# Identity products of TensorE placed in its waits, in a two-block network on one core

## What is computed

```
# first block, per layer
mod = silu(c) @ w_mod + b_mod                 # shifts, scales and gates, 6 x 1024 columns
h   = x * (1 + scale1) + shift1               # latent and context tokens
y   = mixer(h)                                # layer 0: mLSTM scan and attention, layer 1: gated linear attention
x   = layernorm(ALPHA * x + gate1 * y)
f   = peer(x * (1 + scale2) + shift2)         # product-key experts, 16384 of them
x   = layernorm(ALPHA * x + gate2 * f)
# second block, per layer
h   = rmsnorm(x, g_pre)
x   = x + rmsnorm(mixer2(h), g_post)
x   = x + rmsnorm(ffn(rmsnorm(x, g_ffn_pre)), g_ffn_post)
```

## Time and profile before

| | us |
|---|---|
| median of 3 runs | 4111.04 |
| the three runs | 4105.31, 4111.04, 4121.91 |
| the profiled execution, its time | 4121.83 |
| its span, first to last instruction | 4120.1 |
| PE busy in the span | 3940.9 (96%) |
| DVE busy | 3032.1 (74%) |
| ACT busy | 1819.4 (44%) |
| mean granted clock of PE | 0.978 |

### The profile page before, as it was taken

The page is one execution under the profiler, slowest core; times in us unless marked ns, Lnnn a source line. Parts: engine busy times, 40 slices in busy tenths (PEclk is TensorE's granted clock), DMA queues, the critical chain, the costliest instruction groups (busy, mean ns, idle before and its releaser), DMA issues. The chain is left out here.

```text
span 4120.1 us, 66400 instructions
## 1 busy us (share of the span) xinstructions
PE 3940.9 (96%) x25970; PEld 3522.6 (85%) x25970; DVE 3032.1 (74%) x6800; ACT 1819.4 (44%) x2915; POOL 5.9 (0%) x18
## 2 busy tenths in 40 slices
PE   7997999999999999999989999999999789998999
PEld 5766999998888999988868789999888787988798
DVE  3556797778886877788975469777888767756875
ACT  3343444443334444443434344444333544555454
POOL 0000000000000000000000000000000000000000
PEclk8998999999999999999988999999999899999999
DMA  5143575566666865567641247655677422442143
GB/s 214 54 164 123 176 230 180 169 198 240 244 229 257 318 240 168 172 231 256 244 178 70 86 173 231 202 169 176 234 247 245 158 100 77 184 174 107 72 169 143
DMA packets 121684, 752.17 MB, mean 183 GB/s; under 512 B 15712, under 2 KB 17248, under 8 KB 56992
## 3 DMA queue, kind: packets, MB, share of 16 engines
q1 hardware_dynamic: 121376, 747.93, 51.8%
HBM read 693.88 MB, written 54.00 MB: 182 GB/s over the span
## 5 line engine op out<-in xcount | busy, mean ns | idle before, releaser
L1863 DVE TENSOR_TENSOR expert_ring_low<-expert_ring,expert_high 128x1024 fp32r<-128x1024 f32 x768 | 936.1, 1220 | 244.1 <-ACT expert_high L2097 243.8
L2097 ACT ACTIVATE expert_high<-expert_ring 128x1024 fp32r<-128x1024 f32 x768 | 811.9, 1057 | 629.4 <-PE ps L2036 626.0
L2005 PE MATMUL ps<-peer_hT_high_peer,expert_high 128*128 128x256 f32 x3072 | 882.2, 287 | 1.2 <-DVE expert_ring_low L1863 1.0
L2007 PE MATMUL ps<-peer_hT_high_peer,expert_ring_low 128*128 128x256 f32 x3072 | 861.0, 280 | 0.0
L2006 PE MATMUL ps<-peer_hT_low,expert_high 128*128 128x256 f32 x3072 | 860.8, 280 | 0.0
L2005 PEld LDWEIGHTS ps<-peer_hT_high_peer,expert_high 128*128 128x128 f32 x3072 | 583.2, 190 | 3.3 <-DVE expert_ring_low L1863 2.5
L2006 PEld LDWEIGHTS ps<-peer_hT_low,expert_high 128*128 128x128 f32 x3072 | 584.0, 190 | 0.0
L2007 PEld LDWEIGHTS ps<-peer_hT_high_peer,expert_ring_low 128*128 128x128 f32 x3072 | 578.8, 188 | 0.0
L2036 PE MATMUL ps<-expert_high,weighted_high 128*128 128x512 f32 x1536 | 474.5, 390 | 5.8 <-DVE weighted_low L1893 5.8
L2036 PE MATMUL ps<-expert_high,weighted_low 128*128 128x512 f32 x1536 | 474.4, 390 | 0.0
L2036 PE MATMUL ps<-expert_ring_low,weighted_high 128*128 128x512 f32 x1536 | 473.8, 390 | 0.0
(11 more groups left out here) (645 smaller groups left out, 7086.7 us busy)
## 6 DMA issues: line engine op xcount, KB each, us to landing
expert_ring<-in_peer_u SPq DMA_DIRECT2D x192, 1024.0 KB, 5.3
expert_ring<-in_peer_v SPq DMA_DIRECT2D x192, 1024.0 KB, 4.9
gelu_peer<-gelu_out SPq DMA_DIRECT2D x186, 256.0 KB, 5.5
gelu_in_peer<-gelu_peer SPq DMA_DIRECT2D x93, 512.0 KB, 5.7
weight_ring<-in_ffn_w_up SPq DMA_DIRECT2D x22, 2048.0 KB, 7.4
weight_ring<-in_w_in SPq DMA_DIRECT2D x14, 2048.0 KB, 7.4
weight_ring<-in_w_mod SPq DMA_DIRECT2D x12, 2048.0 KB, 7.3
weight_ring<-in_peer_wq SPq DMA_DIRECT2D x12, 2048.0 KB, 7.3
```

The costliest lines, as they stand in the source:

```text
L1863: dve.tensor_tensor(piece(low, n), piece(raw, n), high[:, n % LEAD, :].bitcast(F32), ALU.subtract).then_inc(low_done, 1)
L2005: pe.matmul(o, b[:, s], hT_h[:, c, :], start=(c == 0), stop=False)
L2007: mm = pe.matmul(o, lo[:, s], hT_h[:, c, :], start=False, stop=(c == DC - 1))
L2097: act.activation(high[:, n % LEAD, :], piece(raw, n), ACT.Identity).then_inc(high_done, 1)
```

## The change

A helper `keep_going` is added. It issues n products of the identity with itself, 128 by 128 by 128 in float32, each with start and stop set, into the first 128 columns of a PSUM bank whose content nobody reads any more. It is called on TensorE's list at these places:

- in `Modulation`, 8 before each unit's wait for its transfer, 40 more before the last unit, and 4 after the last sums (8 x 4 + 40 + 4 = 76);
- in `transpose_in`, after the transposes and a wait for the first chunk's copies: 58 in both "h1" stages, 34 in "hn";
- in `Mlstm.weighted`, before the last pair's wait for its weights: 50; and after the weave of `mixer_ab`: 44;
- in `MixOut`, at the end of TensorE's list: 22 per tile, that is 88 with four tiles and 44 with two;
- in `peer_experts`, at the end where `end.cols` isn't empty (two of the three): 86;
- in `rms_in`, as its only TensorE work: 40.

Nothing is removed or reordered otherwise.

```diff
@@ -323,7 +323,13 @@
-def transpose_in(nc, G, name, src, tiles, dst, scale=None, shift=None, loads=(), whole=None, moves=()):
+def keep_going(pe, G, bank, n):
+
+    for _ in range(n):
+        pe.matmul(G.ps[:, bank, 0:P], G.ident[:, :], G.ident[:, :], start=True, stop=True)
+
+
+def transpose_in(nc, G, name, src, tiles, dst, scale=None, shift=None, loads=(), whole=None, moves=(), idle=0):
@@ -342,7 +348,9 @@
                         mm = pe.transpose(ps[:, c, k * P:(k + 1) * P], src(t, c), G.ident[:, :])
                     mm.then_inc(turned, 1)
-
+                if idle:
+                    pe.wait_ge(v_out, pairs)
+                    keep_going(pe, G, 0, idle)
@@ -416,6 +424,7 @@
             def parts(u):
+                keep_going(pe, G, 0, 8)
                 ws.wait_landed(pe, self.u0 + u)
@@ -441,9 +450,12 @@
             parts(0)
             for u in range(1, N):
+                if u == N - 1:
+                    keep_going(pe, G, 0, 40)
                 parts(u)
                 sums(u - 1)
             sums(N - 1)
+            keep_going(pe, G, 0, 4)
@@ -1047,6 +1059,9 @@
                 yield self.t(n) + 5.4 + 0.9 * t
                 if t == 0:
+                    if n == len(self.combos) - 1:
+                        pe.wait_ge(S.qk_out, 4 * H_M)
+                        keep_going(pe, self.G, 2, 50)
                     pe.wait_ge(S.w_ready, 4 * (n + 1))
@@ -1349,6 +1364,8 @@
     def tensor(self, pe):
         yield from merged(self.turn(pe), self.rows(pe), self.products(pe))
+        pe.wait_ge(self.S.cat_low, 2 * len(self.tiles))
+        keep_going(pe, self.G, 4, 22 * len(self.tiles))
@@ -1504,7 +1521,7 @@
             hT_at = nc.sbuf_base - 2 * DC * TOK * 4
             transpose_in(nc, G, "h1", lambda t, c: G.x[:, t, c * P:(c + 1) * P], [0, 1, 2, 3], hT,
-                         scale=lambda c, q: G.mod[:, DC + c, q:q + 1], shift=lambda c, q: G.mod[:, c, q:q + 1])
+                         scale=lambda c, q: G.mod[:, DC + c, q:q + 1], shift=lambda c, q: G.mod[:, c, q:q + 1], idle=58)
             highs = sbuf(nc, "pieces_high", [P, 2, DC, PIECE], F32R)
@@ -1607,6 +1624,8 @@
                     weave(in1.tensor(pe), gates.tensor(pe), rope.tensor(pe), attention.tensor(pe), scan.tensor(pe),
                           mods.tensor(pe))
+                    pe.wait_ge(S.qk_out, 4 * H_M)
+                    keep_going(pe, G, 2, 44)
@@ -2083,6 +2102,9 @@
             products_v(N_KEYS - 2, 1).then_inc(pv_done, 1)
             products_v(N_KEYS - 1, 1).then_inc(pv_done, 1)
+            if end.cols:
+                pe.wait_ge(rows_out, 2 * len(end.cols))
+                keep_going(pe, G, 0, 86)
@@ -2880,6 +2902,10 @@
                    loads=loads) as (
                 block, squared, step_sem, ms_ready, rms_ready, scale_ready, scaled):
+            @block.tensor
+            def _(pe):
+                keep_going(pe, G, 0, 40)
+
             @block.vector
@@ -2911,7 +2937,7 @@
         g = sbuf(nc, "norm_cols", [P, DC], F32)
         rms_in(nc, G, xn, [(g[:, :], G.d[key]), *loads])
-        transpose_in(nc, G, "hn", lambda t, c: xn[:, t, c * P:(c + 1) * P], [0, 1], hT, scale=lambda c, q: g[:, c:c + 1])
+        transpose_in(nc, G, "hn", lambda t, c: xn[:, t, c * P:(c + 1) * P], [0, 1], hT, scale=lambda c, q: g[:, c:c + 1], idle=34)
```

## The result

The changed kernel takes 4165.38 us (median of 4 runs, 4161.06 to 4169.27) against 4109.62 for the kernel before (4 runs, 4105.31 to 4121.91). The ratio is 1.0133, with a 95% interval of 1.0114 to 1.0151: slower by 56 us, where +52 was forecast. The profiled execution took 4169.27 us. Two executions of the kernel before in a later job took 5436 and 8108 us, at a mean granted clock of 0.67 and 0.62; they are in the slow state and left out of every comparison.

A forecast was written before the change was run, and what follows sets the result against it. The prediction took the kernel to be bound by TensorE, busy in 96% of the span. Overruns less clock gains summed to +50.2 us, 4161.2 from the median 4111.04; it took 4163 us, range 4138 to 4184.

The forecast's parts named there:

- One product costs 0.224 us: Each added identity product is two TensorE records of 0.112 us at full clock; 664 products take 149 us.
- the eight overruns: Products outlasting their waits delay stages at the edited places, from +2.9 us in `load_x` to +16.4 from third peer to "hn".
- The scan's line: Scan of `mixer_ab`: groups of 50 and 44 products overrun their waits; together +6.7 us, start of `mix_out` included.
- the -0.5: Start of `mix_out` in `mixer_ab`: better clock gains only 0.5 us, ScalarE being nearly full there.
- Rival 3: Overrun half hidden, other engines starting the next stage while PE finishes: 4153 us; chance 0.87 together with the forecast.
- The gains by the clock: Work behind the filled waits runs at full instead of half clock; 16 us taken, about 19 counted full.
- `mixer_c`'s `In1` (-2.2): Behind "h1" of `mixer_c`, 4.36 us of work at 0.50 would run at full clock, gaining 2.2 us.
- `mixer_2` (-2.0): Start of `mixer_2`: 4.04 us of work at 0.50 would run at full clock, gaining 2.0 us.
- The stretch of 23.89 us: From 2167.36, PE busy at 0.50, costing 11.9 us; read as coming and going, its products untouched by the change.
- Rival 1: At one record, 0.112 us, per product all groups fit their waits and only gains stay: 4095 us; chance 0.10.
- Rival 2: Identity products don't hold the clock, each taking about 0.4 us, gains lost: about 4297 us; chance 0.03.
- The signs: Profile after: about 1328 records of 0.112 us, PE ending stages 6 to 8 us after DVE, clock 1.00 behind edited places.

The follow-up runs named there:

- e3_double: The changed kernel with every group of identity products at twice its length (1328 products): 4314.77 us, ratio 1.0484 to the kernel before.
- wide pair: e9_wide_after compared with e5, which differ by the change alone, both with gate products reading 128 rows: 54.1 us apart.
- e9_wide_after: The changed kernel with `mixer_c`'s eight gate products reading 128 rows, zero-padded, in place of 17: 4161.89 us, ratio 1.0097 to the kernel before.
- e8_h1_only: The kernel before with the 58 identity products in both "h1" stages and nothing else: 4124.58 us, ratio 1.0015.
- e2_one_record: The changed kernel with its 664 identity products issued as transposes, one record each: 4112.05 us, ratio 0.9987 to the kernel before.
- e7: The changed kernel with 128-row gate products, groups cut to their waits, and 8 products added at the start of `In1`: 4100.34 us, ratio 0.9955 to the kernel before.
- e1: The changed kernel with every group of identity products halved (332 in all): 4111.72 us, ratio 0.9988 to the kernel before.
- e4: The kernel before with only the 86 products at the ends of the second and third peer: 4127.08 us, ratio 1.0027.
- e10: The changed kernel with each identity product multiplying 2 columns in place of 128, same number of products: 4277.15 us, ratio 1.0382 to the kernel before.
- e5: The kernel before with `mixer_c`'s eight gate products reading 128 rows, zero-padded, in place of 17: 4107.82 us, ratio 0.9970.
- e6: The changed kernel with halved groups of identity products and gate products reading 128 rows: 4104.38 us, ratio 0.9967 to the kernel before.

## Why the prediction was right

**The price.** "One product costs 0.224 us" held: 1328 records at 0.112 us, and e3_double adds 149.4 us for 664. The row of L2045 in the earlier trace rows was the right one to go by. By the Trainium skill's page "TensorE: Matmul & The Clock Gate" (Back-to-back issue gap), 128 columns in bf16 stand 56 ns apart by themselves and about 81 ns apart in a stream of weight loads and products. The trace has 112 ns for a record in float32, and two records.

**The overruns.** A stage waits until PE has worked off its list; that was the step from 664 products to places, and the eight overruns came within 0.4 us. The scan's line is 0.9 below the prediction, but not by its overruns: from its last pair to the first instruction of `mix_out` the delay grows by 7.15 us (7.2 in the wide pair), and the terms without the -0.5 give 7.2. It is the start of `mix_out` that gave back 1.3 and 1.4 us where I took 0.5: its 16 transposes take 1.94 us in place of 3.41 and are not held up by ScalarE.

```profile
334.78 3.41 PE L1323 MATMUL ps<-ident,cat 128*128 128x128 f32 x16 [5.76 <-PEq L120]
```

```profile
350.19 1.94 PE L1338 MATMUL ps<-ident,cat 128*128 128x128 f32 x16 [0.30 <-PEq L120]
```

Rival 3, that the overrun is half hidden, falls by the timeline: the next stage starts 0.25 to 0.30 us behind PE's last product at each place read, and e3's extra products cost their full price.

**The gains by the clock** were the mis-sized term. I took 16 us; of those behind "h1", `mix_out` and "hn" 3.7 us didn't come in the one pair of the ledger and 4.4 in the other, and `mix_out`'s start gave 0.9 more. At `mixer_c`'s `In1` (-2.2) the clock falls again behind the wait of 3.05 us between the last product and the first of `In1`: 0.61 in the 4.36 us behind it, where the earlier trace rows has 0.50. At `mixer_2` (-2.0) the two pairs differ. In the changed kernel's profile the clock is kept (1.00), but the products wait for the splits on DVE, which come 1.14 us apart, so that a faster PE mostly waits more and 0.5 us are gained. In e9_wide_after the clock fell again behind the same wait, and 0.05 us are gained:

```profile
3294.62:3297.26 2.64, 0.00 (x0) 1.00 0.10 13
3297.26:3301.30 4.04, 4.04 (x20) 0.58 0.60 211
```

The prediction had counted half of the time at half clock without asking whether PE, made faster, would find its operands, and it had taken for granted that the clock lasts through the 2.4 us ahead of a stage's first product. At `mixer_ab`'s `In1` the clock stayed at 1.00 behind a wait of 2.65 us, and 2.35 of 2.55 came; in e8_h1_only it fell there behind the same wait. In e2_one_record it stayed at 1.00 behind the 3.04 us at `mixer_c`, and 2.0 of the 2.2 us came. So the length of the wait alone doesn't decide it, and what does isn't shown. Where the products reach the first one of the next stage, as in e7, the gain comes at `mixer_c` too.

**The stretch of 23.89 us** was read as something that comes and goes. It does: before's runs in the three later jobs lie either near 4109 or near 4122, 12 to 13 us apart, where 11.9 were worked out for it. But the reason given, that it isn't touched by the change, was only half of it. The identity products don't remove it (the profiles of the changed kernel, e1 and e2 have it; those of e3, e4, e8 and e10, with the same narrow products, don't). With the wide products none of the four profiles has it, and in all 12 runs of e5 the upper group is gone. It isn't shown that every run of the upper group has the stretch, since only the profiled execution is seen. The mean granted clock of the other executions fits it: 0.977 to 0.980 in the 21 upper runs of e5's job and 0.979 to 0.982 in the five lower ones, and 23.89 us at half clock are worth 0.003.

**The rivals.** Rival 1, the products fit, is what e1 and e2 show: with half the records the loss is gone. Its 4095 was too low, by the gains above and the stretch; e7, with the stretch removed, reached 4100. Its cause, one record per product, was wrong. Its limit of about 0.13 us a product was read from the wrong group: the tightest is not 34 products in 4.63 us but the 48 before the last unit of `load_x`, in 5.68 us, which is 0.118. Rival 2, the clock falls in spite of them, didn't happen with 128 columns; e10 shows that it can with 2, and its 4277 stands near the 4297 worked out for it. Part of that is chance: a product took 0.43 us at half clock and not 0.40, and a quarter of the records ran at full clock.

**The signs.** The records, their distance, the release by PE and the later start of the next stage (7.1 us behind DVE's end in "h1" and 8.5 at the third peer, for 6 to 8) came as written. Two signs didn't: the clock behind `mixer_c`'s "h1" is 0.61, and `normed_T`'s first stage takes 9.5 us and not 12. For that stage 40 products and a drain are 9.2 us by the prediction's own price, and the sum has them so.

**Luck, and what stays open.** The profile of after regains 7.4 us between the start of `mixer_2` and the end, where nothing was changed. PE worked 27 us at half clock there, and 41 in the profile of before. The same part gave 3.5 to 5.6 us in e1, e2, e3, e6 and e7, 2.2 to 2.5 in e5, e8 and e9, and 1.3 to 1.5 in e4 and e10; I can't say what decides it. It helped the number: the profiled execution took 4169 where 4172 were worked out for it, and without those 7.4 us it would have been 4177. The base helped as well: 4111.04, from which the 4163 were worked out, was the median of three runs, while 44 of the 60 later ones lie near 4122. What doesn't rest on luck is the sum: 50.2 us predicted, 54.1 between e9 and e5. By the ledger's wide column the difference is 4.1, which is the gains that didn't come (4.4) with what came above and below the other terms.

## What to carry to other kernels

Fill a wait only with what fits into it with the drain. The engine's queue must be empty at the stage's end, so every product too many costs its whole price (0.224 us here), while the clock gives back at most half of the few microseconds behind the wait, where it runs at half. Count records from a row of the same type and form ahead of the edit, let the filler reach up to the first product that it is to serve, and ask whether that product's operands will be there. Before filling idle time at all, look for stretches where the engine is busy and slow: widening eight products gave more (13 us at their place, in the executions that had the stretch) than all the filling at its best (7.5 us).

## What the hardware showed beyond that

- The clock fell while PE was busy without a break: 23.89 us at 0.50 beside products of 17 rows, gone with 128 rows of which the added ones are zeros; and 297 us of work at 0.50 with products of two columns. The runs don't tell what property of a product the clock goes by; zeros in the added rows were enough. With the narrow products the stretch comes in some executions and not in others.
- A 128x128 float32 product of 2 columns and one of 128 columns need the same 0.112 us a record at full clock. A transpose of the same size is one record of 0.109 us and kept the clock at 1.00 just as the products did (e2).
- The profiles with added products or transposes of 128 columns have 20 waits of 2.64 to 3.11 us between the last of them and the next stage's first product, at the two `In1` and at `mixer_2`. Behind nine the clock stayed at 1.00. Behind eleven it fell, to 0.58 to 0.72 over the first 4 to 5 us. Both happened at each of the three places.
- What the clock was worth here: 7.5 us of 4108, 0.18%, with the waits filled to measure. The Trainium skill's page "TensorE: Matmul & The Clock Gate" (Part 1) puts the cost of the ramp to full clock below 1% of a typical kernel's span; for the ramps behind these waits the runs agree.
